# Stick-breaking attention summed by parts: the scan is multiplied by row steps of V, and the differences of the scan are no longer formed

## The reference, cut to what matters

```python
z = jnp.einsum('bqhd,bkhd->bhqk', qb, k) * scale
strict = key_idx[None, :] < q_idx[:, None]
log_beta = jax.nn.log_sigmoid(z)
log_1mb = jnp.where(strict, jax.nn.log_sigmoid(-z), 0.0)
later = lax.cumsum(log_1mb, axis=3, reverse=True) - log_1mb
a = jnp.where(strict, jnp.exp(log_beta + later), 0.0)
return jnp.einsum('bhqk,bkhd->bqhd', a, v)
```

## Time and profile before

| | |
|---|---|
| profiled execution, its own time | 2860.66 us |
| its span | 2858.8 us |
| mean granted TensorE clock (share of full) | 0.996 |
| PE busy | 2788.6 us (98%) |
| DVE busy | 1894.1 us (66%) |
| ACT busy | 1471.7 us (51%) |
| POOL busy | 861.9 us (30%) |
| DMA moved | 559.42 MB, mean 196 GB/s |

### The profile page before, as it was taken

The page is one execution under the profiler, slowest core; times in us unless marked ns, Lnnn a source line. Parts: engine busy times, 40 slices in busy tenths (PEclk is TensorE's granted clock), DMA queues, the critical chain, the costliest instruction groups (busy, mean ns, idle before and its releaser), DMA issues.

```text
span 2858.8 us, 51825 instructions
## 1 busy us (share of the span) xinstructions
PE 2788.6 (98%) x19192; PEld 2449.8 (86%) x19192; DVE 1894.1 (66%) x2800; ACT 1471.7 (51%) x2572; POOL 861.9 (30%) x947
## 2 busy tenths in 40 slices
PE   7999999999999999999999999999999999999998
PEld 6888778878888877777899999998889998999886
DVE  6214430087777777777577877787478877878656
ACT  5112221177777666666455545554355555655444
POOL 1832222066776786776002221111100000011110
PEclk9999999999999999999999999999999999999999
DMA  5489897466554523520559999999757784899984
GB/s 195 137 191 225 211 231 170 119 156 148 113 133 107 119 60 75 119 82 16 199 164 331 323 284 289 283 285 290 197 165 235 241 252 157 256 328 300 253 230 158
DMA packets 303337, 559.42 MB, mean 196 GB/s; under 512 B 32272, under 2 KB 70160, under 8 KB 301968
## 3 DMA queue, kind: packets, MB, share of 16 engines
q1 hardware_dynamic: 262768, 463.06, 51.0%
q0 software_dynamic: 39072, 92.30, 17.4%
q10 hardware_dynamic: 1312, 1.64, 0.2%
HBM read 449.91 MB, written 197.13 MB: 226 GB/s over the span
## 4 chain that ended last, share of the span: by engine, by line
PE 70%; DVE 4%; DMA 2%; ACT 2%; issue 1%; POOL 1%; SPq 0%; DVEq 0%; ACTq 0%; POOLq 0%
PE f_ps L2507 26%; PE f_ps L2391 19%; PE h_z L714 5%; PE h_o L1003 5%; PE h_z L717 5%; PE h_t L981 4%; PE h_o L939 3%; PE h_t L924 2%; DVE f_wlo L1880 1%; DMA f_wraw<-sums_scratch 1%; PE h_z L716 1%; DVE h_negmax L1178 1%; PE f_ps L2431 0%; PE f_ps L2417 0%; DVE f_xsum L2093 0%
## 5 line engine op out<-in xcount | busy, mean ns | idle before, releaser
L1880 DVE TENSOR_TENSOR f_wlo<-f_wraw,f_whi 128x512 fp32r<-128x512 f32 x834 | 574.7, 690 | 234.1 <-ACT f_whi L1873 232.3
L1873 ACT ACTIVATE f_whi<-f_wraw 128x512 fp32r<-128x512 f32 x834 | 520.8, 627 | 393.8 <-PE f_ps L2507 254.3
L2507 PE MATMUL f_ps<-f_hi_s,f_whi 128*128 128x256 f32 x1408 | 391.2, 278 | 7.1 <-DVE f_up L2232 7.1
L2507 PE MATMUL f_ps<-f_lo_s,f_whi 128*128 128x256 f32 x1408 | 391.7, 278 | 0.0
L2507 PE MATMUL f_ps<-f_hi_s,f_wlo 128*128 128x256 f32 x1408 | 389.8, 277 | 0.0
L1364 POOL TENSOR_TENSOR h_work<-h_more 128x1024 f32<-128x1024 f32 (+7 forms) x192 | 264.7, 1395 | 115.6 <-DVE h_more L1264 115.6
L2507 PE MATMUL f_ps<-f_hi_a,f_whi 128*128 128x256 f32 x1056 | 292.0, 276 | 1.0 <-DVE f_second L2232 1.0
L2507 PE MATMUL f_ps<-f_hi_a,f_wlo 128*128 128x256 f32 x1056 | 291.6, 276 | 0.0
L2507 PE MATMUL f_ps<-f_lo_a,f_whi 128*128 128x256 f32 x1056 | 291.6, 276 | 0.0
L2507 PEld LDWEIGHTS f_ps<-f_hi_s,f_whi 128*128 128x128 f32 x1408 | 264.4, 188 | 8.8 <-DVE f_wlo L1880 4.4
L1264 DVE TENSOR_TENSOR_SCAN h_more<-h_z,h_zero 128x1024 f32<-128x1024 f32 (+7 forms) x128 | 231.7, 1812 | 59.4 <-ACT h_z L1096 56.9
(11 more groups left out here) (203 smaller groups left out, 6448.2 us busy)
## 6 DMA issues: line engine op xcount, KB each, us to landing
f_wraw<-in_w_stream SPq DMA_DIRECT2D x394, 256.0 KB, 4.3
f_wraw<-sums_scratch SPq DMA_DIRECT2D x352, 256.0 KB, 4.8
sums_scratch<-in_w_stream POOLq DMA_DIRECT2D x132, 256.0 KB, 5.4
act_scratch<-f_act SPq DMA_DIRECT2D x88, 256.0 KB, 4.0
combined_acts<-f_act SPq DMA_DIRECT2D x88, 256.0 KB, 5.2
f_wraw<-down_sums SPq DMA_DIRECT2D x88, 256.0 KB, 3.5
f_piece<-combined_acts SPq DMA_DIRECT2D x88, 256.0 KB, 3.1
down_sums<-in_w_stream POOLq DMA_DIRECT2D x66, 256.0 KB, 6.3
```

The costliest lines, as they stand in the source:

```text
L1873: act.activation(w_hi[ring][:], w_raw[ring][:], ACT.Copy).then_inc(S["hi_split"], 1)
L1880: dve.tensor_tensor(w_lo[ring][:], w_raw[ring][:], w_hi[ring][:].bitcast(F32), ALU.subtract).then_inc(S["lo_split"], 1)
L2507: mm = pe.matmul(outs[i], w[ring][:, col], a[name][:, c, :], start=(c == 0 and m == 0), stop=(c == 3 and m == 2))
```

## The change: what it does, and the diff

- POOL's difference per step goes. The scan writes straight into work[e % 4], the four-slot ring that the transposes read; where a scan goes on from an earlier piece it begins with column 0 of the work tile two steps back.
- ACT's gate writes to one of two SBUF tiles (`gated`, in `more`), and the scan reads it there.
- The evacuation of the transposes adds a bias of -1 (Identity in place of Copy), which makes c - 1.
- V is replaced by v_step = v shifted down by a row, less v. For each of the four pairs SP loads the shifted rows with two more DMAs (load_shifted), behind V and before the last query loads, and POOL clears one row and subtracts once (step_values), at a time that `stepped_at` gives: after unit 62 of diff for pair 4, after breaking(6), (23) and (40) for pairs 5, 6 and 7. The apply of a pair's first piece waits for it.
- The three two-bank PSUM tiles (two of z, and t_bank) become a ring of three. From piece 3 on every block of scores and every turn takes the next one in turn, and waits for the gate or the evacuation that last read it.
- PE's order in a piece is now both steps' scores of piece i, both turns of piece i - 1, lay, and the whole apply of piece i - 2. Turning lags one piece in place of two, applying two in place of three, closing three in place of four. `ahead()` now stands between the two turns of the last piece.
- Buffers: lambdas and their product lie in `squares`, the shadow buffers are gone, two 16x128-column tiles for v_step are new.

```diff
+def load_shifted(sp, v, v_scratch, p, done):
+
+    first = rows_of(p)[2]
+    rows = v_scratch[p // DIFF_PAIRS, :, first:first + COLS].rearrange("(k p) n -> p k n", p=P)
+    sp.dma_start(v[1:P], rows[0:P - 1]).then_inc(done, 16)
+    sp.dma_start(v[0:1, 1:TOK_TILES, :], rows[P - 1:P, 0:TOK_TILES - 1, :]).then_inc(done, 16)
...
+        v_step = [sb("h_vstep0", [P, TOK_TILES, COLS])]
...
-        width = [SEQ + 1, HALF_SEQ - P + 1]
-        stick = [[more[:, m * width[0]:(m + 1) * width[0]] for m in range(2)],
-                 [more[:, behind_probs + m * width[1]:behind_probs + (m + 1) * width[1]] for m in range(2)]]
-
-        z = [memory.enter_context(nc.psum_tensor(f"h_z{s}", [P, CHUNK], F32)) for s in range(2)]
-        t_bank = memory.enter_context(nc.psum_tensor("h_t", [P, CHUNK], F32))
+        gated = [more[:, k * CHUNK:(k + 1) * CHUNK] for k in (2, 3)]
+        v_step.append(more[:, behind_probs:behind_probs + TOK_TILES * COLS].rearrange("p (t n) -> p t n", n=COLS))
+
+        ring = [memory.enter_context(nc.psum_tensor(f"h_z{s}", [P, CHUNK], F32)) for s in range(3)]
         o_bank = [memory.enter_context(nc.psum_tensor(f"h_o{s}", [P, GROUP], F32)) for s in range(2)]
...
-        def shadow(seg, m):
-
-
-            buffer, end = (stick[0][m], SEQ if seg["opens"] else HALF_SEQ) if seg["two"] or not seg["at"] \
-                else (stick[1][m], HALF_SEQ - P)
-            return buffer, end - seg["tiles"] * P, end
+
+        scores_in, turned_in, held_by, place = {}, {}, [None, None, None], 0
+        for i in range(len(pieces) + 1):
+            for m in range(2):
+                if i < len(pieces):
+                    slot = m if i < 3 else place % 3
+                    scores_in[2 * i + m], held_by[slot] = (slot, held_by[slot]), ("gated", 2 * i + m + 1)
+                    place += 1
+            for m in range(2):
+                if i:
+                    slot = m if i < 3 else place % 3 if i < len(pieces) else 2
+                    turned_in[2 * (i - 1) + m], held_by[slot] = (slot, held_by[slot]), ("evacuated", 2 * (i - 1) + m + 1)
+                    place += 1
+
+        def stepped_at(p):
+
+
+            return diff_units + 1 + pieces_through(p - 2) + 6 if p > DIFF_PAIRS else units_through(p - 2) + 11
...
                 load_values(sp, v_sb[s], v_scratch, p, values[s])
+                if p >= DIFF_PAIRS:
+                    load_shifted(sp, v_step[s], v_scratch, p, values[s])
                 load_queries(sp, q_main[s], qk_scratch, p, INNER[0], INNER[1], INNER[0], inner[s])
...
-                if e < 2:
+                slot, holder = scores_in[e]
+                if holder is None:
                     pe.wait_ge(D["exped"], diff_steps)
                 else:
-                    pe.wait_ge(S["scanned"], e - 1)
-                score_matmuls(pe, z[m], query_of(s), k_st[s], m, t["segs"], (ident_bf, strict)).then_inc(S["scored"], 1)
+                    pe.wait_ge(S[holder[0]], holder[1])
+                score_matmuls(pe, ring[slot], query_of(s), k_st[s], m, t["segs"], (ident_bf, strict)).then_inc(S["scored"], 1)
 
             def stick_turn(step):
                 e = step["e"]
-                pe.wait_ge(S["multiplied"], e + 1)
-                if e:
-                    pe.wait_ge(S["evacuated"], e)
+                slot, holder = turned_in[e]
+                pe.wait_ge(S["scanned"], e + 1)
+                if holder is None:
+                    pe.wait_ge(D["evacuated"], diff_units)
                 else:
-                    pe.wait_ge(D["evacuated"], diff_units)
+                    pe.wait_ge(S[holder[0]], holder[1])
                 for j in range(CHUNK_TILES):
-                    mm = pe.transpose(t_bank[:, j * P:(j + 1) * P], work[step["slot"]][:, j * P:(j + 1) * P], ident[:])
+                    mm = pe.transpose(ring[slot][:, j * P:(j + 1) * P], work[step["slot"]][:, j * P:(j + 1) * P], ident[:])
                 mm.then_inc(S["transposed"], 1)
...
+            def stick_apply(t):
 
 
                 s = t["p"] % 2
-                if half == 0:
-                    if t["r"] == 0 and t["c"] == 0:
-                        pe.wait_ge(values[s], 16 * (t["p"] // 2 + 1))
-                    pe.wait_ge(S["evacuated"], t["steps"][1] + 1)
+                if t["r"] == 0 and t["c"] == 0:
+                    pe.wait_ge(S["stepped"], t["p"] - DIFF_PAIRS + 1)
+                pe.wait_ge(S["evacuated"], t["steps"][1] + 1)
...
-                            mm = pe.matmul(o_bank[use % 2][own, at * P:(at + 1) * P], v_sb[s][:, seg["key_tile"] + j, own],
+                            mm = pe.matmul(o_bank[use % 2][own, at * P:(at + 1) * P], v_step[s][:, seg["key_tile"] + j, own],
...
-                cur, turning, applying, closing = piece_at(i), piece_at(i - 2), piece_at(i - 3), closing_at(i - 4)
-                if cur is None and turning is None:
-                    pe.wait_ge(S["scanned"], len(sticks))
-                    ahead()
+                cur, turning, applying, closing = piece_at(i), piece_at(i - 1), piece_at(i - 2), closing_at(i - 3)
                 for m in range(2):
                     if cur is not None:
                         stick_scores(cur, m)
+                for m in range(2):
                     if turning is not None:
                         stick_turn(sticks[turning["steps"][m]])
-                    if applying is not None:
-                        stick_apply(applying, m)
-                    if m == 0 and closing is not None:
-                        lay(closing)
+                    if turning is pieces[-1] and m == 0:
+                        pe.wait_ge(S["evacuated"], len(sticks) - 2)
+                        ahead()
+                if closing is not None:
+                    lay(closing)
+                if applying is not None:
+                    stick_apply(applying)
...
-                act.activation(z[e % 2][:], z[e % 2][:], ACT.Sigmoid, scale=-1.0).then_inc(S["gated"], 1)
+                if e >= 2:
+                    act.wait_ge(S["scanned"], e - 1)
+                act.activation(gated[e % 2][:], ring[scores_in[e][0]][:], ACT.Sigmoid, scale=-1.0).then_inc(S["gated"], 1)
...
+                if e == 0:
+                    act.wait_ge(S["zero_ready"], 2)
...
-                act.activation(attn_t[step["buf"]][:], t_bank[:], ACT.Copy).then_inc(S["evacuated"], 1)
+                act.activation(attn_t[step["buf"]][:], ring[turned_in[e][0]][:], ACT.Identity, bias=minus_one[:]).then_inc(S["evacuated"], 1)
...
-                cur, turning, closing = piece_at(i), piece_at(i - 2), closing_at(i - 4)
+                cur, turning, closing = piece_at(i), piece_at(i - 1), closing_at(i - 3)
                 if closing is not None:
                     lift(closing)
                 for m in range(2):
                     if cur is not None:
                         gate(cur["steps"][m])
+                for m in range(2):
                     if turning is not None:
                         stick_evacuate(sticks[turning["steps"][m]])
-                    if m == 0 and closing is not None:
-                        settle(closing)
+                if closing is not None:
+                    settle(closing)
...
-                m = e % 2
+                m, held = e % 2, work[sticks[e]["slot"]]
                 dve.wait_ge(S["gated"], e + 1)
-                if e >= 2:
-                    dve.wait_ge(S["multiplied"], e - 1)
+                if e >= 4:
+                    dve.wait_ge(S["transposed"], e - 3)
                 for seg in t["segs"]:
-                    buffer, a, b = shadow(seg, m)
                     begin = 1.0
                     if not seg["opens"]:
-                        begin = buffer[:, b:b + 1]
+                        begin = work[sticks[e - 2]["slot"]][:, 0:1]
                         dve.wait_ge(S["scanned"], e - 1)
-                    done = dve.tensor_tensor_scan(buffer[:, a:b][:, ::-1], z[m][:, cols_of(seg)][:, ::-1],
+                    done = dve.tensor_tensor_scan(held[:, cols_of(seg)][:, ::-1], gated[m][:, cols_of(seg)][:, ::-1],
                                                   zero[:].to_broadcast([P, seg["tiles"] * P]), begin, ALU.mult, ALU.add)
...
-            def difference(e, t):
-                if e >= 4:
-                    pool.wait_ge(S["transposed"], e - 3)
-                elif e == 0:
-                    pool.wait_ge(D["combined"], diff_units)
-                pool.wait_ge(S["scanned"], e + 1)
-                for seg in t["segs"]:
-                    buffer, a, b = shadow(seg, e % 2)
-                    done = pool.tensor_tensor(work[sticks[e]["slot"]][:, cols_of(seg)], buffer[:, a + 1:b + 1], buffer[:, a:b], ALU.subtract)
-                done.then_inc(S["multiplied"], 1)
+            def step_values(p):
+
+
+                s = p % 2
+                pool.wait_ge(values[s], 16 * DIFF_PAIRS // 2 + 48 * (p // 2 - DIFF_PAIRS // 2 + 1))
```

(14 more changed lines are left out.)

47 lines of the change are left out of this document (16 added, 31 removed).

## The result

| | before | after |
|---|---|---|
| median of the runs, us | 2862.48 (4 runs) | 2959.84 (4 runs, 2956.88 to 2971.34) |
| ratio, 95% interval | | 1.0342, 1.0305 to 1.0379 |
| profiled execution: time, span, us | 2860.66, 2858.8 | 2956.88, 2955.0 |
| granted clock, mean | 0.996 | 0.977 |

The change costs 97 us where 20 us of gain were forecast. The page of the kernel after answers to the earlier trace rows: PE's share of the span falls from 98% to 94%, and in the chain that ended last a new name stands second.

The account below looks back on a forecast made before the run. PE, busy 98% of the span, was taken to bound the kernel. Blocks -23.5, ramp and end -3.5 and POOL's row step +7.5 summed to -19.5 us: 2841.6 against the median, range 2829 to 2854.

Parts of the forecast that it names:

- Part 4: POOL's four row steps: pair 4's waits for its shifted rows and delays PE; +7.5 us, bounds 1.5 and 10.
- pairs 5 to 7 at 0: Stick-breaking stage: POOL's row steps wait 10 to 35 us for loads, only normalizations queue behind; cost 0.
- Part 1: PE's products in longer blocks per piece: saves 0.345 us a piece, times 68, -23.5 us; bounds 0 and 30.
- Rival D: PE's blocks: no gain from them, as the TensorE page's rule leads to; 2865 us, chance 0.05.
- Part 2: Steady pieces: gates, scans, evacuations and ACT's other work stay hidden beside PE's 5.7 us unmasked piece; cost 0.
- C: Three-bank PSUM ring binds: a late gate stops PE each piece, half the block gain goes; 2853 us, chance 0.12.
- E: DVE's scan from memory becomes the bound through sharing with POOL; at 1.5 times its length about 2920 us, chance 0.06.
- Part 3: Ramp and end of stick-breaking attention: 3.1 and 1.8 us ahead, less 1.4 counted elsewhere; -3.5 us, bounds 0 and 6.
- The slower case: DVE's scan reading memory becomes the bound; about 2920 us, chance 0.06.
- The sum: Whole kernel: -23.5 - 3.5 + 7.5 = -19.5 us, giving 2841.2 us, or 2841.6 against the median.

Follow-up runs that it names:

- even load: Changed kernel with V's shifted rows loaded as tiles 1 to 15 into all 128 partitions, then tile 0's 127 rows; 2849.16 us, ratio 0.9963.
- one input: Kernel of the even load with POOL's subtraction replaced by a product with 1, so output is not the layer's; 2844.48 us in one run.
- the quarters: Kernel of the even load with POOL's row step cut into four subtractions of 512 columns, in four following, later slots; 2841.67 us, ratio 0.9934.

## Why the prediction was wrong, by its own steps

**Part 4 is the step that failed, twice.** "the shifted rows are as large again (1 MB) behind it in a queue that is 0.95 full at 248 GB/s: 4.2 us more". The bytes were right, the rate was not: one of 16 engines, 19 GB/s, about 53 us. The rate was taken from a load into 128 partitions and put on one into 127; the trace of before has none of the latter, and the stated bounds (1.5 to 10) came from when the rows land, not from how fast such a DMA may be. PE's wait was 57.55 us in place of 7.5, by the very chain laid out (totals, reciprocal, maximum, exponential, scores):

```profile
942.03 0.58 PE L722 MATMUL h_z<-h_k,h_qmain 128*128 128x256 f32 x1 [57.55 <-ACT h_more L1070]
```

With the even load the same working holds: the rows were there at 878.97, some 6 us behind V by V's 17.6 us to landing, the step waited 7.90 us and took 4.49 (3.8 said), PE 9.84. To that come some 2 us that the working left out: the granted clock was 0.54 from 880 to 887 us, while PE stood, and 0.81 over the 10 us after it, which lose 1.9 by that (an estimate). The stage is 12.3 us longer than before's, 11.6 of them from the 48th block of apply products on.

The second failure: pairs 5 to 7 at 0, because "only normalizations queue behind them, which nobody needs soon". DVE's sum of squares waits for that normalization, and DVE works in order, with the scans of the next piece behind it:

```profile
1080.03 0.69 DVE L1290 TENSOR_REDUCE h_ssumsq<-h_squares 128x8 f32<-128x512 f32 x1 [20.00 <-POOL h_out L1387]
1080.63 5.26 DVE L1282 TENSOR_TENSOR_SCAN h_work<-h_more,h_zero 128x1024 f32<-128x1024 f32 x2
```

```profile
1082.96 0.47 PE L1004 MATMUL h_z<-ident_sb,h_work 128*128 128x128 f32 x1 [15.51 <-DVE h_work L1282]
```

POOL waited 75.9, 82.5 and 56.1 us for the three loads, and pieces 15, 32 and 49 came out 19.1, 37.1 and 5.4 us longer than before's, 61.6 in all. The waits of 10 to 35 us that were forecast did come with the even load (34.52, 36.40 and 15.22 us), and in the kernel "one input", which has them too (34.99, 37.57 and 14.79), PE waits for nothing between pieces 4 and 67. So the claim held for a wait of that size and not for what happened; it named no size from which it would break, and no run here finds it.

**Part 1, the blocks: right.** Two starts of pieces with masks are 5.95 us apart, 0.35 under before's 6.30 for its like pieces without lay (0.345 said):

```profile
1151.43 0.50 PE L722 MATMUL h_z<-h_k,h_qmain 128*128 128x512 f32 x1
...
1153.64 1.91 PE L1004 MATMUL h_z<-ident_sb,h_work 128*128 128x128 f32 x16
1155.48 1.97 PE L1023 MATMUL h_o<-h_attn_t,h_more 128*64 128x128 f32 x32
1157.38 0.50 PE L722 MATMUL h_z<-h_k,h_qmain 128*128 128x512 f32 x1
```

The turns take 1.84 and the apply 1.90 between starts, as summed (1.83, 1.90); over 63 pieces 21.3 us, which for 68 would be 23.0, in place of 23.5. Rival D is out, and with it the rule of the Trainium skill that the prediction set against this part ("TensorE: Matmul & The Clock Gate", section "Step-by-step: what each phase is for"): reordering the same products moves 0.34 us a piece.

**Part 2, what must stay hidden: its sizes right, one rival passed over.** 61 of 72 scans of 1024 columns stay at 2.26 to 2.31 us with the even load; the others, up to 3.07, stand beside POOL's normalizations. Gates take 1030 ns (1008 to 1020 said), evacuations 1112 (1020 said, hidden), and no table load was added. The ring of three banks doesn't bind, as PE waits for no gate and no evacuation between pieces 4 and 67: C is out. E was priced as a scan slow all the time, and it isn't. But its cause is real where POOL works: "POOL's work in this stage, though, nearly vanishes" overlooked the row step of Part 4, which stands in the same stage and holds the scans for 4.5 us. That is 9.1 us in the even load's kernel.

**Part 3, ramp and end: mis-sized.** The end is right: scores of piece 67 to the projection 16.45 us with the even load (17 said, 22.5 before). The ramp isn't: "piece 4's scores start at 938.2 in place of 937.57", 26.5 us behind piece 0's, and it was 31.3. PE has four waits there, 3.97 us together where the working had about 1.1, for gates and, last, for an evacuation that stands behind the last differential unit:

```profile
918.96 1.06 PE L1005 MATMUL h_z<-ident_sb,h_work 128*128 128x128 f32 x8 [0.50 <-ACT h_more L1119]
921.08 1.06 PE L1005 MATMUL h_z<-ident_sb,h_work 128*128 128x128 f32 x8 [1.05 <-ACT h_more L1119]
927.06 2.12 PE L1005 MATMUL h_z<-ident_sb,h_work 128*128 128x128 f32 x16 [0.15 <-ACT h_more L1119]
935.32 0.80 PE L723 MATMUL h_z<-h_k,h_qmain 128*128 128x512 f32 x1 [2.27 <-ACT h_attn_t L1130]
```

Behind the last of them the granted clock is 0.57 from 935 to 939 us, which is 1.7 us more, an estimate from that figure. Ramp and end together gained 0.7 us (47.6 to 46.9) in place of 4.9.

**The rivals.** None had the outcome. The slower case was given to the scan; the mechanism that decided was in Part 4, whose own worst case was 10 us. With the load made even and the step in quarters the change gives 0.9934 of before's time, 19 us less. The sum had 19.5 for the change as written, but that the two agree is luck: the forecast is made of -23.5, -3.5 and +7.5, and the quarters' kernel has -20.3 in the steady part, nothing at ramp and end, and +1.5 at pair 4's step.

## What to carry to other kernels

Before costing a DMA by its bytes, ask how many engines it is dealt to: here 127 partitions in place of 128 turned some 6 us into 53, and cutting the same bytes otherwise took it back. Of a wait put on an in-order engine, follow what stands behind it to the end of the chain, and say at what length of wait the slack ends; moving the wait was worth 91 us where mending the load was worth 111. And when an operand moves from PSUM to memory, look for every POOL operation in the same stretch: a long one beside a two-input VectorE instruction stops it (9.1 us here), and in four parts it cost 1.0.

## What was not expected of the hardware

- One DMA of 1016 KB into 127 partitions runs at 19 GB/s with a DMA share of 0.07, one engine's worth, and the issue of the next holds SP for 54.30 us; 896 KB into 112 partitions, from partition 1 too, land 18.9 us after their issue, behind V's 1024 KB with 16.9.
- VectorE's two-input scan and POOL's operations from memory, of two inputs or of one, exclude each other for their whole length (0.93 us becomes 5.26 or 2.61), where a scan that read PSUM kept its 2.29 us. The profile books the wait as busy time.
- The granted clock dips in some stretches of some executions (0.84 from 819 to 839 us with the quarters, 1.00 with the even load), and the projections' stage takes 559 to 577 us; single executions differ by more than 10 us with it. Why is open.
